# A decoder layer on one core: order of loads at the start of the down stage, and order of copies in the first gate matrix

## The chip, the core and the metric

The kernel runs on one core of a Trainium2 chip. The metric is device time in microseconds (us). The engines named below are TensorE (PE, with PEld for its weight loads), VectorE (DVE), ScalarE (ACT), GpSimd (POOL) and SyncE (SP), which here only issues DMAs; SPq is its queue.

## The reference

One inference step of a one-layer hybrid decoder: 1024 prompt tokens and 32 sample tokens (1056 columns in the kernel), width 1024. Attention and a recurrent mixer come first, then a gated feed-forward part of width 2816. Only that part is touched:

```python
def conv_ffn(h, buf, w_gate, w_up, conv_w, conv_b, w_down):
    T = h.shape[1]
    a = h @ w_gate
    ext = jnp.concatenate([buf.astype(a.dtype), a], axis=1)
    c = conv_b + sum(conv_w[j] * ext[:, j:j + T] for j in range(CONV_W))
    y = (jax.nn.silu(c) * (h @ w_up)) @ w_down
    return y, ext[:, -(CONV_W - 1):]
...
xp = xp + mixer_out(...)
y, cbuf_p = conv_ffn(rms_norm(xp, norm2_g[l]), buf0, w_gate[l], w_up[l], conv_w[l], conv_b[l], w_down[l])
xp = xp + y
```

## The kernel before, in words

Everything is float32. Each operand of a product is split into a high part (ScalarE, a copy to a shorter format) and a low part (the rest: VectorE for tokens, GpSimd for weights), and each product is three matmuls: high by high, high by low, low by high. Each engine works through its own list in the order written; semaphores join them.

The feed-forward part is computed in block products of Strassen's kind (Winograd's form): seven products in place of eight. There are 11 groups of 256 hidden features, and each has a gate matrix and an up matrix of seven items (`matrix`, L2386 and on). An item runs for two halves `z` of 264 columns; its result stays in one of three pairs of PSUM banks, "a", "b", "c" (roles `acababa`). `copies` (ScalarE) takes the result of items 0, 2 and 3 out to SBUF; `c11`, `c22` and `c12` (VectorE) add it to other banks, and `bank_free` holds TensorE until a bank may be written: item 5 waits for the copy of item 3 (`w5_ready`), item 6 for `c22`.

**The gate seam** is the first group's gate matrix. There the token operands of items 2 to 6 are still being made (`x_high` on ScalarE, `x_low` on VectorE; steps 20 to 23 are B22 for item 5, steps 24 to 27 are T4 for item 6, from `make_t4`), and so is the norm's root: `log_of(1)`, `log_of(2)` read PSUM banks, `root` follows, and VectorE waits for it (`rb_ready`) before it scales the gates. TensorE's transpose of the old gates behind item 5 waits for all three logs (`ln_ready`), since it writes one of their banks. GpSimd's next work waits for `make_t4`.

**The down stage** has 154 steps `s` (`B_STEPS`), 11 to a run `r`, 14 runs; run `r` is product `p = r // 2`, half `z = r % 2`. A step is 12 matmuls of 264 columns. It needs a weight quad (one for two steps, loaded by `down_weights`, split by ScalarE and GpSimd) and a token piece: `acts_in(s)` loads it into one of 8 stages, `act_high(s)` (ScalarE) and `act_low(s)` (VectorE) split it into one of 8 operand buffers. In runs 2 and 3 a piece has two parts (264 KB in place of 132), and VectorE forms their difference first (`t_sum`). Both engines work 6 steps ahead (`AHEAD`), VectorE's `t_sum` 8 steps. SyncE issues the pieces 12 steps ahead, each behind the low part of the piece 8 before it (`tl_ready`). At the end of a run VectorE adds the PSUM banks to the residual (`evict`). The residual `acc` lies where the operands T3 and T4 were, so it comes back from memory (`residual_back`) behind the last up matrix. The last group's products are stored and read back (`products`, `p_stored`), and the sums of its down weights are formed from three loaded blocks (`sum_sources`, then `down_sums` on VectorE, then `sums_out`).

Of the kernel before, what the change touches and what calls it, by code (L numbers as in the profile page):

```python
# [29 lines left out]
TT = T + NS  # L30
NT = T // P
NPC = 3
PW = TT // NPC
# [1823 lines left out]
GROUPS = FC // G2  # L1857
HF = TT // 2
ZW = HF // 2
KH = KC // 2  # L1860
# [95 lines left out]
def tail(nc, io, keep, room, at):  # L1956
# [7 lines left out]
    with ExitStack() as ctx:  # L1964
        sb, ps, sem = open_memory(nc, ctx, keep["sems"])
# [103 lines left out]
        th_ready, tl_ready, b_ready = sem("th_ready"), sem("tl_ready"), sem("f_b_ready")  # L2069
        r_in = [sem(f"r_in{n}") for n in range(2)]  # L2070
        be_ready, yt_ready, ye_ready, yd_ready = sem("be_ready"), sem("yt_ready"), sem("ye_ready"), sem("yd_ready")
# [16 lines left out]
        with nc.Block() as block:  # L2088
            @block.sync
            def _(sp):  # L2090
# [68 lines left out]

                def residual_back(side):  # L2160
                    if side == 0:
                        sp.wait_ge(res_stored[0], 16)
                    else:
                        sp.wait_ge(res_stored[2], 16 * KH)
                        sp.wait_ge(res_stored[3], 16 * KH)
                    sp.wait_ge(res_stored[1], 16)
                    cols = slice(side * HF, (side + 1) * HF)
                    sp.dma_start(acc[:, :, cols], io["x_d"][:, :, cols]).then_inc(r_in[side], 16)

# [71 lines left out]
                sp.wait_ge(p_ready, p_use(MATS - 1, 6, 1))  # L2241
                residual_back(0)
                acts_in(8), acts_in(9)
                sum_sources(GROUPS - 1)
                sp.wait_ge(p_stored, 16 * GROUPS)
                acts_in(10), acts_in(11)
                residual_back(1)
                sums_out(GROUPS - 1)
                for s in range(B_STEPS):
                    r, f = divmod(s, GROUPS)  # L2250
                    if s + 12 < B_STEPS:
                        acts_in(s + 12)
                    q = quad_at(s)
                    if s >= 4 and q is not None and q + 4 < B_QUADS:
                        down_weights(q + 4)
                    if r - 1 in DONE and f == 9:
                        outputs(r - 1)
# [233 lines left out]
            def _(act):  # L2491
# [197 lines left out]
                def gate_matrix(m, g, first):  # L2689
# [12 lines left out]
                    if first:  # L2702
                        for i in range(20, 24):
                            x_high(i)
                        log_of(1), log_of(2), root(slice(PW, TT))
                        copies(m, g, 0, 3, True, False)
                        for i in range(24, 28):
                            x_high(i)
                    next_quad(m, g, 0, 2, False)
                    if not first:  # L2710
# [50 lines left out]
                for s in range(B_STEPS):  # L2761
                    r, f = divmod(s, GROUPS)
# [15 lines left out]
            def _(dve):  # L2778
# [171 lines left out]
                def group(g, first, link, last=False):  # L2950
# [5 lines left out]
                    if first:  # L2956
                        for i in range(20, 24):
                            x_low(i)
                        for j in range(KH):
                            make_t4(j)  # L2960
                        for i in range(24, 28):
                            x_low(i)
                        dve.wait_ge(rb_ready, 2)
                    c22(m, 0, gates[1])
                    dve.wait_ge(c22_ready, m * 2 + 2)
# [37 lines left out]
                def evict(r, block, j):  # L3003
                    h, side = BLOCKS[r // 2][block]
                    z = r % 2
                    if r in (0, 2) and j == 0:
                        dve.wait_ge(r_in[r // 2], 16)
                    if r >= 4 and block == 0 and j == 0:
# [7 lines left out]
                for s in range(B_STEPS):  # L3016
# [3 lines left out]
                    if s + AHEAD < B_STEPS:  # L3020
                        act_low(s + AHEAD)
                    if s == 2:
                        down_sums(GROUPS - 1)
# [132 lines left out]
```

## Time and profile before

| | us |
|---|---|
| median of three runs | 1471.75 (1470.19 to 1478.22) |
| the profiled execution | 1464.73 |
| its span | 1463.0 |
| TensorE busy | 1402.4 |
| VectorE busy | 997.1 |
| ScalarE busy | 712.7 |
| GpSimd busy | 630.7 |

Mean granted TensorE clock: 0.983 of full speed. The gate and up matrices run from about 733 us to 1215 us, the down stage from there to 1457 us. Matmuls overlap, so the start of one to the start of the next (0.12 us for 264 columns at full clock) is what counts, not the length shown.

### The profile page before, as it was taken

The numbers are of one execution on the slowest core, as the hardware profiler recorded it, in microseconds if no ns is written. First come the engines' busy times: TensorE is split into PE (matmuls) and PEld (weight loads), VectorE is DVE, ScalarE is ACT, GpSimd is POOL, SyncE is SP. The second block draws the span as 40 slices with busy tenths as digits, with TensorE's granted clock in tenths as the row PEclk, the third lists the DMA queues.
The fourth block names the chain that finished last, engine by engine and source line by source line (L and its number), as shares of the span: only waits on it lengthen the run. The fifth ranks groups of instructions, "written<-read, shape, count | busy, mean of one in ns | idle before, by whom it ended". The sixth has DMA issues, their size and how long they took to land.

```text
span 1463.0 us, 27919 instructions
## 1 busy us (share of the span) xinstructions
PE 1402.4 (96%) x10382; PEld 1329.4 (91%) x10382; DVE 997.1 (68%) x1698; ACT 712.7 (49%) x1412; POOL 630.7 (43%) x408
## 2 busy tenths in 40 slices
PE   6999999999999998999988999999999997999998
PEld 5888989798979897869988999999999997999998
DVE  6558555855585458756499777777788775976952
ACT  5537544745564456364364444434444443544452
POOL 0000300030003000423149889999999973544840
PEclk9999999999999899999999999999999998999999
DMA  8221103110311030846311443343223348966762
GB/s 276 94 73 30 39 22 103 29 45 17 103 43 30 17 102 16 249 134 213 118 50 31 132 130 131 103 130 131 81 95 116 131 154 293 316 186 192 248 208 76
DMA packets 174952, 171.41 MB, mean 117 GB/s; under 512 B 9351, under 2 KB 144908, under 8 KB 174860
## 3 DMA queue, kind: packets, MB, share of 16 engines
q1 hardware_dynamic: 173614, 169.38, 36.9%
q8 instruction: 59, 0.97, 0.3%
q10 hardware_dynamic: 1246, 0.79, 0.2%
q14 instruction: 33, 0.27, 0.1%
HBM read 125.75 MB, written 44.39 MB: 116 GB/s over the span
## 4 chain that ended last, share of the span: by engine, by line
PE 47%; DVE 4%; issue 2%; DMA 1%; SPq 0%; POOL 0%; ACT 0%; POOLq 0%; DVEq 0%; ACTq 0%
PE f_up L2324 8%; PE f_up L2326 8%; PE f_up L2325 8%; PE f_gp L2324 7%; PE f_gp L2326 7%; PE f_gp L2325 7%; PE f_dn L2324 1%; PE f_dn L2325 1%; PE f_dn L2326 1%; DMA m_raw<-w_out 1%; DMA f_ksum<-w_down 1%; DVE f_conv L2920 1%; DVE f_conv L2913 0%; DVE f_conv L2916 0%; DVE f_act L2926 0%
## 5 line engine op out<-in xcount | busy, mean ns | idle before, releaser
L143 PE MATMUL z_ps<-h_hi,w_hi 128*128 128x352 f32 x600 | 202.5, 337 | 0.0
L145 PE MATMUL z_ps<-h_hi,w_lo 128*128 128x352 f32 x600 | 194.7, 324 | 0.0
L144 PE MATMUL z_ps<-h_lo,w_hi 128*128 128x352 f32 x600 | 194.3, 324 | 0.0
L2291 POOL TENSOR_TENSOR f_qlo<-f_raw,f_qhi 128x512 fp32r<-128x512 f32 x88 | 149.2, 1705 | 41.2 <-ACT f_qhi L2585 24.0
L2295 POOL TENSOR_TENSOR f_bring<-f_braw,f_bring 128x512 fp32r<-128x512 f32 x77 | 108.0, 1407 | 106.9 <-ACT f_bring L2616 106.8
L578 POOL TENSOR_TENSOR room<-room 128x1056 f32<-128x1056 f32 x4 | 9.7, 2434 | 321.5 <-ACT room L1235 321.5
L2291 POOL TENSOR_TENSOR f_qlo<-f_sum,f_qhi 128x512 fp32r<-128x512 f32 x66 | 130.4, 1987 | 15.7 <-ACT f_qhi L2585 15.7
L2926 DVE TENSOR_TENSOR f_act<-f_stage,f_act 128x264 fp32r<-128x264 f32 x132 | 88.7, 693 | 58.3 <-ACT f_act L2629 58.3
L143 PEld LDWEIGHTS z_ps<-h_hi,w_hi 128*128 128x128 f32 x600 | 114.3, 191 | 1.8 <-issue 1.3
L144 PEld LDWEIGHTS z_ps<-h_lo,w_hi 128*128 128x128 f32 x600 | 114.8, 191 | 0.3
L145 PEld LDWEIGHTS z_ps<-h_hi,w_lo 128*128 128x128 f32 x600 | 114.1, 190 | 0.0
L573 POOL TENSOR_TENSOR room<-room 128x512 f32<-128x512 f32 (+1 forms) x28 | 30.4, 1087 | 179.4 <-DVE room L1465 104.8
L2629 ACT ACTIVATE f_act<-f_stage 128x264 fp32r<-128x264 f32 x132 | 54.8, 422 | 107.0 <-PE f_gp L2326 37.4
L1079 ACT ACTIVATE room<-z_ps 128x352 f32<-128x352 f32 x81 | 37.2, 459 | 133.9 <-PE z_ps L145 125.4
L2585 ACT ACTIVATE f_qhi<-f_raw 128x512 fp32r<-128x512 f32 x88 | 54.8, 625 | 84.7 <-PE f_up L2326 44.1
L2324 PE MATMUL f_gp<-f_act,f_bring 128*128 128x264 f32 x231 | 66.7, 289 | 0.0
L2325 PE MATMUL f_gp<-f_act,f_bring 128*128 128x264 f32 x231 | 66.2, 287 | 0.0
L2326 PE MATMUL f_gp<-f_act,f_bring 128*128 128x264 f32 x231 | 66.2, 286 | 0.0
L2324 PE MATMUL f_up<-f_act,f_bring 128*128 128x264 f32 x231 | 65.7, 284 | 0.0
L2325 PE MATMUL f_up<-f_act,f_bring 128*128 128x264 f32 x231 | 65.5, 284 | 0.0
L2326 PE MATMUL f_up<-f_act,f_bring 128*128 128x264 f32 x231 | 65.5, 283 | 0.0
L2585 ACT ACTIVATE f_qhi<-f_sum 128x512 fp32r<-128x512 f32 x66 | 41.2, 627 | 37.3 <-PE f_up L2326 31.3
(462 smaller groups left out, 5027.9 us busy)
## 6 DMA issues: line engine op xcount, KB each, us to landing
f_stage<-a_d SPq DMA_DIRECT2D x132, 132.0 KB, 3.1
w_raw<-w_in SPq DMA_DIRECT2D x28, 512.0 KB, 4.0
a_d<-f_u SPq DMA_DIRECT2D x11, 1056.0 KB, 8.8
f_raw<-w_gate SPq DMA_DIRECT2D x22, 512.0 KB, 6.1
f_raw<-w_up SPq DMA_DIRECT2D x22, 512.0 KB, 5.1
f_braw<-w_down SPq DMA_DIRECT2D x44, 256.0 KB, 3.6
f_ksum<-w_down SPq DMA_DIRECT2D x33, 256.0 KB, 3.2
s_d<-f_ksum SPq DMA_DIRECT2D x11, 768.0 KB
```

Of the source, the lines that this page charges most:

```text
L143: nc.tensor.matmul(out, whi[:, k, :], hi[:, k, :], start=(k == 0), stop=False)
L144: nc.tensor.matmul(out, whi[:, k, :], lo[:, k, :], start=False, stop=False)
L145: last = nc.tensor.matmul(out, wlo[:, k, :], hi[:, k, :], start=False, stop=(k == chunks - 1))
L1079: return a(dst[:, piece(n)], bank_of(k)[:, 0:PW], ACT.Copy)
L2291: tt(qlo[i][:, :, :], source(b, i), qhi[i][:, :, :].bitcast(F32), ALU.subtract).then_inc(aw_ready, 1)
L2295: tt(ring[q % SLOTS][:, 1, :, :], braw[q % 8][:, :, :], ring[q % SLOTS][:, 0, :, :].bitcast(F32), ALU.subtract).then_inc(aw_ready, 1)
L2324: mm(out, wh, xh, start=first, stop=False, skip_group_check=goes_on)
L2325: mm(out, wh, xl, start=False, stop=False, skip_group_check=goes_on)
L2326: return mm(out, wl, xh, start=False, stop=last, skip_group_check=goes_on)
L2585: a(qhi[i][:, :, :], source(b, i), ACT.Copy).then_inc(ah_ready, 1)
L2629: a(acts[s % 8][:, 0, :], src, ACT.Copy).then_inc(th_ready, 1)
L2926: v.tensor_tensor(acts[s % 8][:, 1, :], src, acts[s % 8][:, 0, :].bitcast(F32), ALU.subtract).then_inc(tl_ready, 1)
```

## The change

In the down stage, SyncE's list is put in another order: pieces 8 and 9, the wait for the stored products and pieces 10 and 11 come before any residual; the residual comes in four blocks (rows 0 to 3 and rows 4 to 7 of the eight, left and right half) at the head and in steps 5, 12 and 15; the sum sources are loaded in step 1, their sums stored in step 9, and VectorE makes them in its step 5 in place of step 2. The waits of `evict` follow. In the gate seam, ScalarE's copies of item 3 and `x_high` 24 to 27 come before the two logs and the root, and VectorE's `c22` before `x_low` 24 to 27.

```diff
--- before.py
+++ after.py
@@ -2067,7 +2067,7 @@
         braw_in = [sem(f"braw_in{s}") for s in range(8)]
         st_in = [sem(f"st_in{s}") for s in range(STAGES)]
         th_ready, tl_ready, b_ready = sem("th_ready"), sem("tl_ready"), sem("f_b_ready")
-        r_in = [sem(f"r_in{n}") for n in range(2)]
+        r_in = [sem(f"r_in{n}") for n in range(3)]
         be_ready, yt_ready, ye_ready, yd_ready = sem("be_ready"), sem("yt_ready"), sem("ye_ready"), sem("yd_ready")
         y_stored = [sem(f"y_stored{s}") for s in range(YBUFS)]
 
@@ -2157,15 +2157,15 @@
                     else:
                         sp.dma_start(stage[s % STAGES][:, 0, :], io["a_d"][2 * f + (p in (4, 5, 6)), :, cols]).then_inc(st_in[s % STAGES], 16)
 
-                def residual_back(side):
+                def residual_back(h, side):
                     if side == 0:
                         sp.wait_ge(res_stored[0], 16)
                     else:
                         sp.wait_ge(res_stored[2], 16 * KH)
                         sp.wait_ge(res_stored[3], 16 * KH)
                     sp.wait_ge(res_stored[1], 16)
-                    cols = slice(side * HF, (side + 1) * HF)
-                    sp.dma_start(acc[:, :, cols], io["x_d"][:, :, cols]).then_inc(r_in[side], 16)
+                    rows, cols = slice(KH * h, KH * h + KH), slice(side * HF, (side + 1) * HF)
+                    sp.dma_start(acc[:, rows, cols], io["x_d"][:, rows, cols]).then_inc(r_in[2 if h else side], 16)
 
                 def outputs(r):
                     h, tiles = DONE[r]
@@ -2239,15 +2239,22 @@
                 products(GROUPS - 1)
                 down_weights(14)
                 sp.wait_ge(p_ready, p_use(MATS - 1, 6, 1))
-                residual_back(0)
                 acts_in(8), acts_in(9)
-                sum_sources(GROUPS - 1)
                 sp.wait_ge(p_stored, 16 * GROUPS)
                 acts_in(10), acts_in(11)
-                residual_back(1)
-                sums_out(GROUPS - 1)
+                residual_back(0, 0)
                 for s in range(B_STEPS):
                     r, f = divmod(s, GROUPS)
+                    if s == 1:
+                        sum_sources(GROUPS - 1)
+                    if s == 5:
+                        residual_back(0, 1)
+                    if s == 9:
+                        sums_out(GROUPS - 1)
+                    if s == 12:
+                        residual_back(1, 0)
+                    if s == 15:
+                        residual_back(1, 1)
                     if s + 12 < B_STEPS:
                         acts_in(s + 12)
                     q = quad_at(s)
@@ -2702,10 +2709,10 @@
                     if first:
                         for i in range(20, 24):
                             x_high(i)
-                        log_of(1), log_of(2), root(slice(PW, TT))
                         copies(m, g, 0, 3, True, False)
                         for i in range(24, 28):
                             x_high(i)
+                        log_of(1), log_of(2), root(slice(PW, TT))
                     next_quad(m, g, 0, 2, False)
                     if not first:
                         copies(m, g, 0, 3, False, False)
@@ -2958,10 +2965,12 @@
                             x_low(i)
                         for j in range(KH):
                             make_t4(j)
+                        c22(m, 0, gates[1])
                         for i in range(24, 28):
                             x_low(i)
                         dve.wait_ge(rb_ready, 2)
-                    c22(m, 0, gates[1])
+                    else:
+                        c22(m, 0, gates[1])
                     dve.wait_ge(c22_ready, m * 2 + 2)
                     v.tensor_tensor(gates[1][:, right], gates[1][:, right], total[:, right], ALU.mult).then_inc(gr_ready, 1)
                     c12(m, 0, gates[0])
@@ -3003,8 +3012,8 @@
                 def evict(r, block, j):
                     h, side = BLOCKS[r // 2][block]
                     z = r % 2
-                    if r in (0, 2) and j == 0:
-                        dve.wait_ge(r_in[r // 2], 16)
+                    if r in (0, 2, 4) and block == 0 and j == 0:
+                        dve.wait_ge(r_in[r // 2], 32 if r == 4 else 16)
                     if r >= 4 and block == 0 and j == 0:
                         dve.wait_ge(be_ready, e_count(r - 1))
                     dve.wait_ge(b_ready, b_use(GROUPS * r + GROUPS - 1, j))
@@ -3019,7 +3028,7 @@
                         t_sum(s + AHEAD + 2)
                     if s + AHEAD < B_STEPS:
                         act_low(s + AHEAD)
-                    if s == 2:
+                    if s == 5:
                         down_sums(GROUPS - 1)
                     if f == GROUPS - 1:
                         for block in range(len(BLOCKS[r // 2])):
```

## Rows read from the trace of the kernel before

**Rows 1.** The page, part 1: busy us, share, instructions.

```profile
PE 1402.4 (96%) x10382; PEld 1329.4 (91%) x10382; DVE 997.1 (68%) x1698; ACT 712.7 (49%) x1412; POOL 630.7 (43%) x408
```

**Rows 2.** Stretches: us, busy us by engine, clock, DMA share, GB/s.

```profile
1150.00:1200.00 50.00, 50.00 (x413) 49.96 (x412) 40.26 (x52) 22.70 (x44) 44.13 (x25) 1.00 0.33 109
1200.00:1250.00 50.00, 42.02 (x318) 41.16 (x317) 32.63 (x40) 19.56 (x45) 23.24 (x16) 0.90 0.84 279
```

**Rows 3.** TensorE's timeline, down seam: start, length, idle in brackets.

```profile
1218.41 0.36 PE L2324 MATMUL f_dn<-f_act,f_bring 128*128 128x264 f32 x1 [0.40 <-DVE f_act L2926]
...
1231.39 0.56 PE L2324 MATMUL f_dn<-f_act,f_bring 128*128 128x264 f32 x1 [3.99 <-DVE f_act L2926]
...
1237.20 0.56 PE L2324 MATMUL f_dn<-f_act,f_bring 128*128 128x264 f32 x1 [2.83 <-DVE f_act L2926]
...
1239.97 0.42 PE L2324 MATMUL f_dn<-f_act,f_bring 128*128 128x264 f32 x1
```

**Rows 4.** SyncE's queue in the same seam.

```profile
1216.89 0.40 SPq L2119 DMA_DIRECT2D a_d<-f_u  x1
...
1217.90 0.96 SPq L2168 DMA_DIRECT2D room<-x_d  x1
...
1236.73 0.34 SPq L2132 DMA_DIRECT2D s_d<-f_ksum  x1
```

**Rows 5.** Stretches of the seam: TensorE, clock, DMA share, GB/s.

```profile
1230.00:1235.00 5.00, 2.98 (x12) 0.51 1.06 391
...
1220.00:1235.00 15.00, 10.38 (x73) 0.84 1.03 364
1255.00:1275.00 20.00, 20.00 (x167) 1.00 1.02 344
```

**Rows 6.** Chain of waits, weight sums.

```profile
1222.04 10.69 DMA f_ksum<-w_down
1232.76 1.68 DVE f_ksum L2945
...
1236.11 0.60 DVE f_ksum L2948
```

**Rows 7.** DMA issues: count, KB each, us to landing (first: page).

```profile
f_stage<-a_d SPq DMA_DIRECT2D x132, 132.0 KB, 3.1
...
f_stage<-a_d SPq DMA_DIRECT2D x22, 264.0 KB, 4.9
...
room<-x_d SPq DMA_DIRECT2D x2, 2112.0 KB, 12.6
a_d<-f_u SPq DMA_DIRECT2D x1, 1056.0 KB, 5.2
```

**Rows 8.** TensorE's timeline, gate seam.

```profile
764.87 0.56 PE L2324 MATMUL f_gp<-f_b22h,f_qhi 128*128 128x264 f32 x1 [4.32 <-issue]
```

**Rows 9.** ScalarE's timeline, gate seam.

```profile
757.47 2.61 ACT L2556 ACTIVATE f_b22h<-room,vec 128x528 fp32r<-128x528 f32 x4
...
764.40 0.37 ACT L2647 ACTIVATE f_pw<-f_gp 128x264 f32<-128x264 f32 x1
```

**Rows 10.** VectorE's timeline, gate seam.

```profile
752.43 2.56 DVE L2822 TENSOR_TENSOR f_t1l<-f_t1f,f_t1h 128x528 fp32r<-128x528 f32 x4
...
761.08 2.80 DVE L2814 SCALAR_TENSOR_TENSOR room<-room,vec,f_t2f 128x528 f32<-128x528 f32 x4
765.62 6.51 DVE L2822 TENSOR_TENSOR f_t<-room,f_t 128x528 fp32r<-128x528 f32 x4 [1.74 <-ACT f_t L2554]
772.06 0.76 DVE L2887 TENSOR_TENSOR f_gate<-f_gp,f_pw 128x264 f32<-128x264 f32 x2
...
777.30 0.43 DVE L2973 TENSOR_TENSOR f_gate<-f_gp,total 128x264 f32<-128x264 f32 x1 [0.86 <-PE f_gp L2326]
```

**Rows 11.** GpSimd's timeline, gate seam.

```profile
763.96 2.51 POOL L2291 TENSOR_TENSOR f_qlo<-f_raw,f_qhi 128x512 fp32r<-128x512 f32 x2 [17.24 <-DVE room L2814]
```

**Rows 12.** TensorE's timeline, end of the up matrix.

```profile
796.66 0.36 PE L2324 MATMUL f_up<-f_t,f_qhi 128*128 128x264 f32 x1 [1.65 <-DVE f_u L2887]
```

## The prediction

> **What bounds the kernel now.** The page comes first: TensorE is busy for 1402.4 of 1463.0 us [rows 1], so only stretches in which it stands or runs slowly can give time back. The busy time by stretches finds them. From 1150 to 1200 us the engine runs 413 matmuls in 50 us, from 1200 to 1250 only 318 [rows 2]: 95 are missing, at 50/413 = 0.121 us each 11.5 us. A step of the down stage has 12 matmuls, so it takes 1.453 us. TensorE's own timeline places the loss. Step 2 starts at 1218.41; then 3.99 us idle ahead of 1231.39 (step 8) and 2.83 us ahead of 1237.20 (step 9); step 10 starts at 1239.97 [rows 3]. Undisturbed, it would start at 1218.41 + 8 x 1.453 = 1230.0. So 9.9 us are lost by then, with step 10's first two matmuls, still slow, 10.1. Part of it is clock: step 9's 12 matmuls take from 1237.20 to 1239.97, 0.23 us each, and the granted clock is 0.51 then, the lower of the levels 1.2 and 2.4 GHz, after 3.99 us of idling [rows 3, 5].
>
> SyncE's queue says why. At 1217.90 it issues the whole left residual (2112 KB), only then pieces 8 and 9, the sum sources, pieces 10 and 11, and the right residual; pieces 12 on must wait until the weight sums are stored, at 1236.73 [rows 4]. The chain shows the second hold: sources landed after 10.69 us, three VectorE sums up to 1236.71, and only behind them on VectorE the low part of piece 9 [rows 6]. The DMA engines are full all the while: 364 GB/s at a share of 1.03 from 1220 to 1235, and still 344 GB/s at 1.02 from 1255 to 1275 [rows 5].
>
> The second place is the first group's gate matrix: 4.32 us idle ahead of item 5 at 764.87 [rows 8], and a shorter idle stretch ahead of item 6.
>
> **The down stage.** The queue at 1217.9 becomes: pieces 8, 9; the wait for the stored products; pieces 10, 11; a residual block of 1056 KB; then within the loop the sources (s=1), three more blocks (s=5, 12, 15) and the sums' store (s=9). DMAs on SyncE go from 2 residual issues to 4 (0.34 to 0.96 us of issue each [rows 4]); nothing else is added.
>
> Pieces 8 and 9 now have only the product store and 256 KB of weights ahead of them. Behind a queue that short I take the 3.1 us that a small piece has over the whole run [rows 7], counted from the store's landing at 1216.89 + 5.2 = 1222.1 [rows 4, 7] as the late bound: 1225, ahead of step 8 at 1218.41 + 6 x 1.453 = 1227.1. The 3.99 us go, and with them the 2.83 us and the slow clock.
>
> What is late next: the sums. VectorE takes them up after the low part of piece 11, and the low part of piece 12 is queued behind them, then all later ones. Ahead of the last source's landing lie, from 1222.2 on, pieces 10 to 12, one block and 768 KB of sources: 0.41 + 1.08 + 0.79 = 2.27 MB. The first piece lands at 1222.2 + 3.1 = 1225.3, the remaining 2.14 MB at 364 GB/s take 5.9 us: 1231.2. Before, the sums took 1236.71 - 1232.76 = 3.95 us [rows 6]; the shortest of the three took 0.6, so three of that length are 1.8, the other end. GpSimd slows them (below) and works on one weight quad in every two steps, so not all of the time: I take 3.3. With 0.4 us for the low part, step 12 can start at 1234.9 in place of 1218.41 + 10 x 1.453 = 1232.9: a new stall of 2.0 us. Ends: 0 (sources one us early, sums in 2.0 us) and 3.7 (one us late, 3.95 us). The clock should hold: 1.65 us idle at 796.66 left the first matmul at 0.36 us, where a slow one has 0.56 [rows 3, 12].
>
> Next, the DMA engines. The same bytes are moved, and before they were full until 1275. What PE gained must come out of load lead. From step 22 a piece is 264 KB, and VectorE forms a difference of piece n before the low part of piece n-2. So step 25 needs piece 27, the first behind all four blocks. From 1222.2 up to it: pieces 10 to 21, 1.62 MB; 22 to 27, 1.62; blocks 4.33; sources and store of sums 1.57; six weight loads 1.57; in all 10.71 MB, at 364 GB/s 29.4 us. With the first piece landing after 3.1 us and the other 10.57 MB after that it ends at 1222.2 + 3.1 + 29.0 = 1254.3; two VectorE operations on 264 columns (0.4 each, as the additions in [rows 10]) put step 25 at 1255.1. Undisturbed it would be 1251.8, with the 2.0 us stall 1253.8. Before it was 1239.97 + 0.2 + 15 x 1.453 = 1262.0. So the down stage gives 6.9 us. At 391 GB/s, the best five microseconds [rows 5], the stream ends 2 us earlier, the sums' stall rules and it gives 8.2; at 344, 5.2. The lower end is 5, the upper the whole 10.1. I stay at 6.9, on the rate of the same seam. Later steps need 0.27 + 0.13 MB each, 1.1 us at that rate against 1.453: no further stall. The residual's first block is needed at step 10's end and the last at step 54's: both long landed.
>
> The Trainium skill (DMA: Bandwidth & Descriptors, Bandwidth) gives about 358 GB/s as a core's share of HBM and 435 as the fabric's ceiling. The trace lies at 364 to 391, so the first is nearer; by it the stream ends 0.5 us later than in my sum, by the second the DMA engines would bind nowhere.
>
> **The gate seam.** ScalarE is free at 757.47 + 2.61 = 760.1 and then does a table load, two logs, another table load and a root before the two copies at 764.40 [rows 9], 4.3 us in all; item 5 starts as the first is done. Moved ahead, the copies end at 760.75, and item 5 starts behind item 4 at 764.87 - 4.32 = 760.55. It takes 24 x 0.121 = 2.9 us and ends at 763.5. But item 6 needs the low parts of T4. VectorE's make_t4 ends at 761.08 + 2.80 = 763.9 as before; the two c22 additions now come next (0.76 us [rows 10]), then the four lows from 764.6. Their high parts are then there, as ScalarE makes them from 761.8 on instead of after the root. They took 6.51 us at 765.62, while GpSimd worked without pause from 763.96, but 2.56 at 752.43, when it had nothing to do [rows 10, 11]. GpSimd starts on make_t4's signal, which doesn't move, so 6.5 us: 771.1 in place of 772.1. The logs and the root move behind x_high(27), which ends 0.65 us [rows 9] after make_t4, at 764.5; the same 4.3 us put the root's end at 768.8 and the logs' earlier. TensorE's transpose after item 5 waits for the logs, so some 3 us in which only the first T4 rows could run: hidden behind the lows. If item 6 then runs its last 15 matmuls slowly, it ends at 771.1 + 15 x 0.23 = 774.5, against 777.2 before, when VectorE's product waited for it [rows 10]. VectorE, from the end of the lows (c22, before, ended at 772.8) to the start of its last product at 777.30 less 0.86 of waiting, had 3.6 us of work; so 771.1 + 3.6 = 774.7, and with that product's 0.4 it is at 775.1 against 777.7 [rows 10]. Both are 2.6 to 2.7 us ahead. VectorE has no gap from there to 796.66, where TensorE waits 1.65 us for it [rows 12], so its advance is what arrives; with 0.1 off for TensorE's last slow matmuls -2.5. Ends: 0 (something in the next matrix, such as GpSimd's unmoved sums, holds both) and -4.3 (the whole first wait). VectorE needs the root at 771.1, after its end. No table load is added: the order log, root, later activations stays.
>
> The Trainium skill (GPSIMD Engine Reference, Specifications) says that GpSimd shares its SBUF interfaces with VectorE and that instructions with two SBUF inputs contend. The trace agrees (6.51 against 2.56 us). It speaks against expecting the whole 4.3 us: without it the lows would end at 767.2, and PE, waiting for the logs, would gain some 4.
>
> **Sum.** -6.9 - 2.5 = -9.4 us. The profiled execution took 1464.73 us (span 1463.0 and 1.7 around it), so 1455.3 by its own measure. The median of the three runs is 1471.75, 7.0 above it; set against that the forecast is 1462.4. What is under 0.5% (7.4 us) I call no change.
>
> **The rivals.** (A) No new stall: sums and stream come in time, 10.1 + 2.5 = 12.6, 1459.2. For it: the DMA windows reach 391 GB/s; against it: VectorE's order and the full DMA share. 0.17. (B) The DMA engines, not the order, set step 22 on: full from 1218 to 1275 on both sides, so nothing in the down stage comes back, only -2.5: 1469.3. Against it: from 1240 to 1275 SyncE ran ahead of TensorE, so there is lead to spend. 0.12. (C) The gate seam gives nothing, since GpSimd's sums or the transpose's wait for the logs eat it: -6.9, 1464.9. 0.13. (D) Slower: the two late blocks fall among the 264 KB pieces. SyncE may load piece n only after the low part of piece n-8, and that stands six steps behind the difference for piece n-2; so a landing time above 6 x 1.453 = 8.7 us sets the pace. Residuals took 12.6 us to land, the 264 KB pieces 4.9 [rows 7]. Were they at 12.6 for all 22 steps, each six cost 3.9 us more: 14.3, with the slow clock about 18; less 12.6 that is +5: 1477. It decides from 8.7 us on. 0.08. My own case has 0.50, with a range of 1459 to 1466.
>
> **How the numbers follow.** Faster: most of my case, A and a part of C, 0.65. Same: the rest of mine, B and half of C, 0.27. Slower: D, 0.08. The range goes from A less the 1.6 us between the lowest run and the median to just above B, and leaves out D: 1457.5 to 1470.
>
> **What would show it.** Right: no idle ahead of step 8; one gap of about 2 us ahead of step 12, ended by VectorE's low part behind the sums; granted clock 1.00 from 1220 to 1245; landing of 264 KB pieces under 8.7 us; first copies of item 3 at about 760.1, item 6's end near 774.5. Wrong: a gap at steps 20 to 30 of more than 3 us, a half clock there, or a transpose that starts after the T4 lows.

## The result and the profile after

The changed kernel takes 1461.84 us (median of 8 runs, 1454.68 to 1464.88) against 1472.52 us for the kernel before in the same rounds (8 runs, 1468.88 to 1478.22): ratio 0.9931, 95% interval 0.9913 to 0.9949. Two more series of it gave 0.9941 (0.9915 to 0.9967) and 0.9947 (0.9919 to 0.9974). The prediction was 1462.4 us, range 1457.5 to 1470. The profiled execution took 1461.8 us, its span is 1460.0.

The page, part 1, of the kernel after (busy us, share, instructions; compare [rows 1]):

```profile
PE 1408.9 (97%) x10382; PEld 1334.8 (91%) x10382; DVE 1009.4 (69%) x1698; ACT 713.5 (49%) x1412; POOL 639.9 (44%) x408
```

The two profiled spans differ by only 3.0 us, less than the change gives. The reason lies in a half that the change doesn't touch. The stretches (us, busy us and instructions of PE, PEld, DVE, ACT, POOL, then granted clock, DMA share, GB/s), first of before, then of after:

```profile
200.00:300.00 100.00, 96.60 (x655) 85.68 (x655) 62.92 (x140) 62.60 (x129) 6.67 (x6) 1.00 0.20 60
```

```profile
200.00:300.00 100.00, 96.72 (x620) 85.14 (x621) 63.12 (x141) 59.75 (x123) 2.43 (x1) 0.95 0.20 60
1200.00:1250.00 50.00, 46.71 (x368) 46.09 (x367) 37.93 (x50) 21.83 (x48) 26.29 (x18) 0.97 0.83 280
1220.00:1235.00 15.00, 14.60 (x121) 14.42 (x120) 8.74 (x11) 4.11 (x10) 7.41 (x6) 1.00 0.92 299
1235.00:1240.00 5.00, 2.86 (x20) 2.65 (x19) 5.00 (x8) 2.57 (x7) 2.71 (x2) 0.88 1.07 394
1240.00:1245.00 5.00, 5.00 (x34) 5.00 (x34) 3.41 (x8) 2.45 (x6) 2.58 (x2) 0.77 1.04 385
```

From 200 to 300 us this execution was granted 0.95 of the clock and ran 35 matmuls fewer than the one of before (655 and 620). Item 5 of the first gate matrix starts at 766.80 here; before it could have at 764.87 - 4.32 = 760.55 [rows 8]. So everything below is read from marks inside each trace: **the gate part** runs from the moment at which item 5's operands are there and item 4 has ended (its first matmul; where that waited for the copy, less the wait) to step 2 of the down stage, **the down part** from step 2 to the span's end. Before, they are 1218.41 - 760.55 = 457.86 and 1463.0 - 1218.41 = 244.59. After, they are 454.14 and 239.06: 3.7 and 5.5 us less, 9.25 in all.

TensorE's timeline of the kernel after (start, length, idle in brackets; compare [rows 3, 8, 12]):

```profile
766.80 0.36 PE L2331 MATMUL f_gp<-f_b22h,f_qhi 128*128 128x264 f32 x1
...
773.36 0.30 PE L2389 MATMUL f_dn<-ident,f_scr 128*128 128x128 f32 x1 [3.41 <-ACT total L2517]
775.58 0.59 PE L2331 MATMUL f_gp<-f_t,f_qhi 128*128 128x264 f32 x1 [1.07 <-DVE f_t L2829]
777.27 0.59 PE L2331 MATMUL f_gp<-f_t,f_qhi 128*128 128x264 f32 x1 [0.66 <-DVE f_t L2829]
...
800.53 0.36 PE L2331 MATMUL f_up<-f_t,f_qhi 128*128 128x264 f32 x1 [1.58 <-DVE f_u L2894]
...
1220.94 0.36 PE L2331 MATMUL f_dn<-f_act,f_bring 128*128 128x264 f32 x1 [0.40 <-DVE f_act L2933]
...
1237.90 0.39 PE L2331 MATMUL f_gp<-f_act,f_bring 128*128 128x264 f32 x1 [2.14 <-DVE f_act L2933]
...
1263.47 0.36 PE L2331 MATMUL f_dn<-f_act,f_bring 128*128 128x264 f32 x1 [0.35 <-DVE f_act L2933]
```

Item 5 waits for nothing. In the place of its wait stand 3.41 us ahead of the transpose (for ScalarE's logs) and 1.07 and 0.66 us inside item 6 (for the T4 lows). In the down stage the waits ahead of steps 8 and 9 are gone; one of 2.14 us stands ahead of step 12 (1237.90), and step 28 (1263.47) waits a little. The other engines around the two seams, VectorE first (compare [rows 6, 10]):

```profile
770.14 0.77 DVE L2894 TENSOR_TENSOR f_gate<-f_gp,f_pw 128x264 f32<-128x264 f32 x2
770.82 6.39 DVE L2829 TENSOR_TENSOR f_t<-room,f_t 128x528 fp32r<-128x528 f32 x4
...
781.10 0.76 DVE L2982 TENSOR_TENSOR f_gate<-f_gp,total 128x264 f32<-128x264 f32 x2
...
1234.51 0.69 DVE L2952 TENSOR_TENSOR f_ksum<-f_ksum 128x512 f32<-128x512 f32 x1 [3.47 <-DMA f_ksum<-w_down]
...
1236.32 3.98 DVE L2933 TENSOR_TENSOR f_act<-f_stage,f_act 128x264 fp32r<-128x264 f32 x5
...
1257.23 0.43 DVE L2942 TENSOR_TENSOR f_t2raw<-f_stage 128x264 f32<-128x264 f32 x1 [2.37 <-DMA f_stage<-a_d]
```

GpSimd starts its next two operations 0.52 us ahead of VectorE's lows (compare [rows 11]):

```profile
770.30 2.96 POOL L2298 TENSOR_TENSOR f_qlo<-f_raw,f_qhi 128x512 fp32r<-128x512 f32 x2 [17.25 <-DVE room L2821]
```

ScalarE (compare [rows 9]):

```profile
766.32 0.38 ACT L2654 ACTIVATE f_pw<-f_gp 128x264 f32<-128x264 f32 x1
...
768.21 2.69 ACT L2561 ACTIVATE f_t<-room 128x528 fp32r<-128x528 f32 x4 [1.24 <-DVE room L2821]
770.92 1.28 ACT L2517 ACT_TABLE_LOAD   x1
772.21 1.00 ACT L2517 ACTIVATE total<-f_dn,eps 128x352 f32<-128x352 f32 x2
```

And SyncE's queue (compare [rows 4]): pieces 8 and 9 go before the first residual block, and the queue never stands for the sums again.

```profile
1219.43 0.40 SPq L2119 DMA_DIRECT2D a_d<-f_u  x1
...
1220.43 4.82 SPq L2158 DMA_DIRECT2D f_stage<-a_d  x4
1225.34 1.20 SPq L2168 DMA_DIRECT2D room<-x_d  x1
...
1228.31 0.47 SPq L2128 DMA_DIRECT2D f_ksum<-w_down  x1
...
1238.72 0.43 SPq L2132 DMA_DIRECT2D s_d<-f_ksum  x1
...
1242.47 0.40 SPq L2168 DMA_DIRECT2D room<-x_d  x1
...
1246.18 0.47 SPq L2168 DMA_DIRECT2D room<-x_d  x1
```

### The profile page after: what moved, and what is told of

It is laid out like the page before. It is cut to its first block, busy times and chain, and to the rows that moved or that the text cites. A ratio compares the mean times of both kernels' runs of the same rounds, so it can differ in the third digit from the quotient of the medians.

```text
span 1460.0 us, 27925 instructions
## 1 busy us (share of the span) xinstructions
PE 1408.9 (97%) x10382; PEld 1334.8 (91%) x10382; DVE 1009.4 (69%) x1698; ACT 713.5 (49%) x1412; POOL 639.9 (44%) x408
## 4 chain that ended last, share of the span: by engine, by line
PE 44%; DVE 3%; issue 3%; POOL 2%; DMA 2%; ACT 1%; SPq 0%; DVEq 0%; ACTq 0%; POOLq 0%
PE f_up L2331 8%; PE f_up L2333 8%; PE f_up L2332 7%; PE f_gp L2333 6%; PE f_gp L2331 6%; PE f_gp L2332 6%; POOL f_qlo L2298 1%; PE f_dn L2331 1%; PE f_dn L2332 1%; PE f_dn L2333 1%; DMA f_stage<-a_d 1%; DMA f_ksum<-w_down 1%; DVE f_act L2933 0%; DMA a_d<-f_u 0%; DVE f_t2f L2812 0%
## 5 line engine op out<-in xcount | busy, mean ns | idle before, releaser
L2298 POOL TENSOR_TENSOR f_qlo<-f_raw,f_qhi 128x512 fp32r<-128x512 f32 x88 | 152.9, 1748 | 36.8 <-ACT f_qhi L2592 19.1
L2302 POOL TENSOR_TENSOR f_bring<-f_braw,f_bring 128x512 fp32r<-128x512 f32 x77 | 114.4, 1493 | 95.1 <-ACT f_bring L2623 95.0
L2933 DVE TENSOR_TENSOR f_act<-f_stage,f_act 128x264 fp32r<-128x264 f32 x132 | 94.5, 738 | 40.4 <-ACT f_act L2636 40.4
```

Source lines behind the costliest of these rows:

```text
L2298: tt(qlo[i][:, :, :], source(b, i), qhi[i][:, :, :].bitcast(F32), ALU.subtract).then_inc(aw_ready, 1)
L2302: tt(ring[q % SLOTS][:, 1, :, :], braw[q % 8][:, :, :], ring[q % SLOTS][:, 0, :, :].bitcast(F32), ALU.subtract).then_inc(aw_ready, 1)
L2933: v.tensor_tensor(acts[s % 8][:, 1, :], src, acts[s % 8][:, 0, :].bitcast(F32), ALU.subtract).then_inc(tl_ready, 1)
```

## The experiments

Every trace is cut at the same marks, one trace to a kernel. "None listed" means that the trace names no wait there, "one run" that the kernel was run once and has no ratio. The old orders are read as one group, the new ones as another:

| kernel | gate part | down part | idle ahead of step 12 | ratio to before (95%) |
|---|---|---|---|---|
| before | 457.86 | 244.59 | (3.99 + 2.83 earlier) | |
| after | 454.14 | 239.06 | 2.14 | 0.9931 (0.9913 to 0.9949) |
| e1_down | 457.85 | 239.16 | 1.89 | 0.9950 (0.9924 to 0.9977) |
| e2_gate | 453.79 | 245.75 | (3.81 + 2.84 earlier) | 0.9973 (0.9949 to 0.9996) |
| e3_sources_first | 453.64 | 239.37 | none listed | 0.9937 (0.9914 to 0.9961) |
| e4_blocks_late | 455.49 | 235.21 | none listed | 0.9912 (0.9884 to 0.9940) |
| e5_blocks_late_only | 453.5 | 235.60 | 0.84 | one run |
| e6_gpsimd_later | 456.15 | 239.10 | 2.26 | 0.9924 (0.9892 to 0.9955) |
| e7_logs_between | 457.1 | 239.34 | 2.02 | one run |
| e8_c22_back | 456.4 | 239.23 | 0.95 | one run |
| f1_blocks_late_timed | 454.9 | 238.37 | 2.02 | 0.9931 (0.9903 to 0.9960) |
| f2_after_timed | 455.3 | 239.53 | 2.02 | 0.9941 (0.9915 to 0.9967) |
| f3_order_best_timed | 455.8 | 236.09 | 1.08 | 0.9915 (0.9884 to 0.9946) |
| f4_after_paired | 453.6 | 239.21 | 2.15 | 0.9947 (0.9919 to 0.9974) |

### The two halves of the change by themselves: e1_down and e2_gate

The first is the changed kernel with the old gate seam, the second the kernel before with the new one:

```diff
# e1_down
-                        copies(m, g, 0, 3, True, False)
-                        for i in range(24, 28):
-                            x_high(i)
                         log_of(1), log_of(2), root(slice(PW, TT))
+                        copies(m, g, 0, 3, True, False)
+                        for i in range(24, 28):
+                            x_high(i)
...
-                        c22(m, 0, gates[1])
                         for i in range(24, 28):
                             x_low(i)
                         dve.wait_ge(rb_ready, 2)
-                    else:
-                        c22(m, 0, gates[1])
+                    c22(m, 0, gates[1])
```

> Down part of the change alone; the gate seam as before. Measured by the trace from step 2 of the down stage to the end of the span (before 244.6 us, whole change 239.1) and from the last matmul of item 4 in the first gate matrix to step 2 (before 458.1, whole change 454.3). My theory (two independent stalls): 239.1 and 458.1, so 5.5 us off the whole time. Rival (the down stage can only use what the DMA engines leave, and an earlier start of it counts): with the stage starting later by the missing gate gain, the down part would give more, over 7 us.

> Gate part alone; down stage as before. My theory: 454.3 from item 4 to step 2 (3.8 us gained, of which 2.5 by the end of the first up matrix and 1.3 later), 244.6 from step 2 on. Rival: the 1.3 us that came after the first up matrix are chance in how VectorE and GpSimd meet, and the gain is 2.5 (455.6). Whole time 2.5 to 3.8 us below before.

Each keeps its own part to 0.1 to 0.4 us: down alone 239.16, gate alone 453.79. e1's gate part is that of before (457.85). e2's down part is 245.75, 1.2 us above before: with almost the same two waits, its matmuls ran 0.22 us apart up to 1246.66, 6.1 us after the end of the second wait, where before had 3.2 us of that. So the parts add within that spread, and the down stage is the larger. e1's expectation held for both parts, e2's for the gate part; its down part is off by those 1.2 us. Over whole runs e1 is 7.0 and e2 3.2 us below before, where 5.5 and 2.5 to 3.8 were expected. e2's timeline has the old idle places:

```profile
1234.76 0.56 PE L2324 MATMUL f_dn<-f_act,f_bring 128*128 128x264 f32 x1 [3.81 <-DVE f_act L2926]
...
1240.58 0.56 PE L2324 MATMUL f_dn<-f_act,f_bring 128*128 128x264 f32 x1 [2.84 <-DVE f_act L2926]
```

e1's is the more telling one. Its stall ahead of step 12 is 1.89 us with the clock at 1.00, where the changed kernel had 2.14 us and 0.88 and 0.77 behind it; yet its down part is not shorter. What it saved there it lost behind 1260, where step 25 (1265.26) waits 0.69 us, with no such wait in the changed kernel. Step 28 (1270.59) waits as long as there, 0.36 us against 0.35:

```profile
1244.78 0.39 PE L2331 MATMUL f_gp<-f_act,f_bring 128*128 128x264 f32 x1 [1.89 <-DVE f_act L2933]
...
1265.26 0.36 PE L2331 MATMUL f_dn<-f_act,f_bring 128*128 128x264 f32 x1 [0.69 <-DVE f_act L2933]
1270.59 0.36 PE L2331 MATMUL f_dn<-f_act,f_bring 128*128 128x264 f32 x1 [0.36 <-DVE f_act L2933]
```

Step 28 starts 42.55 us after step 2 here and 42.53 us in the changed kernel. Whatever TensorE loses ahead of it, it arrives at the same time. e8 (below) agrees: 0.95 us ahead of step 12, and 239.23.

### Stall or stream: e3_sources_first, e4_blocks_late, e5_blocks_late_only

```diff
# e3: the sources ahead of the first block
+                sum_sources(GROUPS - 1)
                 residual_back(0, 0)
...
-                    if s == 1:
-                        sum_sources(GROUPS - 1)
# e5: the last two blocks behind the 264 KB pieces; e4: both edits
-                    if s == 12:
+                    if s == 33:
                         residual_back(1, 0)
-                    if s == 15:
+                    if s == 36:
                         residual_back(1, 1)
```

> Changed kernel with the sources of the weight sums loaded ahead of the first residual block instead of in step 1. Sources land some 3 us sooner, the sums are made before step 12 needs VectorE, so the 2.1 us idle ahead of step 12 and the slow clock behind it (2.0 us) go in both theories. My theory (DMA engines full, piece 27 is the floor): the same bytes stand ahead of piece 27, which landed 36.3 us after step 2, so a new idle stretch of about 3 us appears at steps 22 to 28 and the stage gains 0 to 1.5 us: 237.6 to 239.1. Rival (only the sums held the stage): all 4.1 us come back, 235.0.

> As the run before, and the last two residual blocks moved from steps 12 and 15 to steps 33 and 36, behind the 264 KB pieces; they are needed at step 54. My theory: with 2.2 MB less ahead of piece 27 the DMA floor is some 6 us lower and all idle of the stage goes: 234.6 to 235.5 from step 2 to the end, 4 us below the changed kernel. Rival (the DMA engines were never a floor): no different from the run before. A third way: the blocks now meet the product 2 and 3 loads and give a stall at steps 36 to 50.

> Changed kernel with only the last two residual blocks moved to steps 33 and 36; the weight sums as in the changed kernel, so the idle stretch of about 2 us ahead of step 12 stays. The run with both moves took 235.2 us from step 2 to the end. If the stall is paid once the stream of pieces is no floor any more: 237.3, or 239.3 where the clock falls after it as it did in the changed kernel (2.14 us idle, clock down to 0.77 over five us) but not in the down-only run (1.89 us idle, clock 1.00). Rival (the floor sits elsewhere, the late blocks gave nothing in the run with both): 239.1 without any fall of the clock.

e3 has no idle time listed ahead of step 12, and its down part is 239.37: removing the stall gave nothing. It came back in four waits at 1255.11 to 1266.81 (0.79, 0.86, 0.68 and 0.37 us, 2.7 in all, where about 3 were expected). e4, with 2.16 MB fewer ahead of piece 27, takes up that piece 30.67 us after step 2 in place of 36.29 (after, e1) and 36.55 (e3): 5.6 to 5.9 us, as 2.16 MB at 377 GB/s would be 5.7. The stall at steps 36 to 50 that its third way named did not come. Its down part is 235.21, close to the 234.5 that before would have without its 10.1 us of loss. The landing times in that stretch, after first (issued between 1219 and 1262), then e4 (1221 to 1262):

```profile
room<-x_d SPq DMA_DIRECT2D x4, 1056.0 KB, 7.8
f_stage<-a_d SPq DMA_DIRECT2D x14, 264.0 KB, 7.9
```

```profile
f_stage<-a_d SPq DMA_DIRECT2D x18, 264.0 KB, 5.1
```

e5 was to lose the step 12 stall of 2 us as before, 237.3 us. It had only 0.84 us of it and 235.60: the size missed, the sign held. The same kernel again (below) had 2.02 us and 238.37. What sets the two apart stands in the traces: how long the first low part behind the sums took. In the tile views it is 1519 ns in after (and 1518 in f1) and 425 ns in e5, and GpSimd's operation beside it goes the other way. First after, then e5:

```profile
L2933 DVE TENSOR_TENSOR f_act<-f_stage,f_act x1: 1519/1519/1519, 1236.3 to 1236.3; 128x264 fp32r<-128x264 f32 x1
L2302 POOL TENSOR_TENSOR f_bring<-f_braw,f_bring x1: 1272/1272/1272, 1236.3 to 1236.3; 128x512 fp32r<-128x512 f32 x1
```

```profile
L2933 DVE TENSOR_TENSOR f_act<-f_stage,f_act x1: 425/425/425, 1224.7 to 1224.7; 128x264 fp32r<-128x264 f32 x1
L2302 POOL TENSOR_TENSOR f_bring<-f_braw,f_bring x1: 1599/1599/1599, 1224.6 to 1224.6; 128x512 fp32r<-128x512 f32 x1
```

In all seven traces with a stall of 1.89 to 2.26 us GpSimd starts 0.04 us ahead of VectorE, and the low part takes 1.51 to 1.52 us. In e5 and e8 GpSimd is 0.03 and 0.01 us ahead, the low part takes 0.43 and the stall is 0.84 and 0.95. So 1.1 us of the stall hang on a few hundredths of a microsecond.

### The gate seam: e6_gpsimd_later, e7_logs_between, e8_c22_back

```diff
# e6: GpSimd behind the T4 lows in place of make_t4
-                pool.wait_ge(t4_ready, KH)
+                pool.wait_ge(xl_ready, len(X_STEPS))
# e7: only the copies ahead of the logs, x_high 24 to 27 behind the root
                         copies(m, g, 0, 3, True, False)
+                        log_of(1), log_of(2), root(slice(PW, TT))
                         for i in range(24, 28):
                             x_high(i)
-                        log_of(1), log_of(2), root(slice(PW, TT))
# e8: only ScalarE's order is new, c22 stays behind the lows
-                        c22(m, 0, gates[1])
                         for i in range(24, 28):
                             x_low(i)
                         dve.wait_ge(rb_ready, 2)
-                    else:
-                        c22(m, 0, gates[1])
+                    c22(m, 0, gates[1])
```

> Changed kernel; GpSimd's next work in the gate seam waits for the four T4 low parts instead of for make_t4. Theory (the two engines slow each other): the four lows take 2.6 us in place of 6.4, so item 6 ends 2 to 4 us sooner; GpSimd starts 3.2 us later and may then hold items 2 and 3 of the up matrix, so of that 1 to 2.5 us are left at step 2 (452 to 453 us from item 5 to step 2, against 454.1, 453.8, 453.6 and 455.5 in the four runs with the gate part). Rival (the lows are slow for themselves, or GpSimd sets the pace after the seam): lows still above 5 us, or no gain or a loss up to 3 us at step 2.

> Changed kernel with ScalarE's logs and root between the copies of item 3 and the four T4 high parts. TensorE's transpose no longer waits 3.4 us for the logs. Theory (that wait was hidden behind the T4 lows, VectorE's chain sets the pace): the first T4 high comes at about 5.2 us after item 5's start instead of 2, the lows start 1.2 us later and the part from item 5 to step 2 is 1.2 us longer. Rival (the transpose's wait is on the path): up to 3.4 us shorter.

> Changed kernel with VectorE's c22 behind the four T4 lows again; ScalarE's order as changed. Theory: item 6 can't start before c22, so its first nine matmuls no longer run between the lows; all 24 run from some 10.2 us after item 5's start at the slow clock, item 6 ends 1.6 us later and step 2 comes 1 to 1.6 us later. Rival (the copies alone made the gain): the same time as the changed kernel, 453.6 to 454.1 from item 5 to step 2.

**e6** shows the contention: with GpSimd idle the same four lows take 2.55 us in place of 6.39. It also shows what is late next. VectorE then waits 1.97 us for the root, and GpSimd's work comes 3.2 us later:

```profile
771.08 2.55 DVE L2829 TENSOR_TENSOR f_t<-room,f_t 128x528 fp32r<-128x528 f32 x4
775.60 1.19 DVE L2975 TENSOR_TENSOR f_gate<-f_gate,total 128x528 f32<-128x528 f32 x1 [1.97 <-ACT total L2521]
```

TensorE starts the up matrix 2.7 us sooner (11.20 us after item 5 in place of 13.94), as expected, but stands 2.60 us at 786.84 in it for ScalarE's copy. The gate part is 456.15, 1.7 us above the mean of the new order, where 452 to 453 was expected: on the time at step 2 the rival held.

**e7** separates the two moves on ScalarE. The copies alone free item 5, but the lows start 5.16 us after item 5 in place of 4.02, since the high parts come behind the root, and they take 6.50 us. The gate part is 457.1: of the mean 3.4 us of the new order 0.8 is left. The loss, 2.7 us against that mean, is more than the 1.2 expected, and not all of it need be the edit's. At the mark of [rows 12] e7 stands 34.81 us after item 5, the old order 36.1, the nine traces of the new order 32.55 to 33.73; behind it come waits that differ from trace to trace (below). The rival (up to 3.4 us shorter without the transpose's wait) fell. Much of the gain lies in the high parts of T4 being made ahead of the logs; how much, one trace doesn't show.

**e8** surprised. Without the two `c22` additions first, the lows took 2.55 us, though GpSimd was working; this time GpSimd's first two operations took 4.74 us where the changed kernel had 2.96. The lows start 0.16 us ahead of GpSimd here and 0.52 us behind it there. VectorE, then GpSimd:

```profile
766.77 2.55 DVE L2829 TENSOR_TENSOR f_t<-room,f_t 128x528 fp32r<-128x528 f32 x4
771.98 0.77 DVE L2894 TENSOR_TENSOR f_gate<-f_gp,f_pw 128x264 f32<-128x264 f32 x2 [2.65 <-ACT total L2521]
```

```profile
766.93 4.74 POOL L2298 TENSOR_TENSOR f_qlo<-f_raw,f_qhi 128x512 fp32r<-128x512 f32 x2 [17.23 <-DVE room L2821]
```

But `c22` stands behind the wait for the root, 8.6 us after item 5's start instead of 3.3, and item 6 waits for `c22`: the gate part is 456.4. So without the move of `c22` 2 us of the 3.4 are lost, by one trace of e8 against the mean of nine of the new order (1 to 1.6 was expected). At the mark of [rows 12] it is less: 34.16 us after item 5, 0.4 to 1.6 us later than the nine. The losses of e7 and e8 add to more than the whole gain (2.7 and 2.0 of 3.4), so they are no shares of it.

### Timed beside each other: f1 to f4

f1 is e5's kernel again, f3 is e4's, f2 and f4 are the changed kernel unedited, each pair in the same rounds.

> The changed kernel with its third and fourth residual block issued in steps 33 and 36 in place of 12 and 15, timed in five rounds; its one run so far cannot be set apart from its undisturbed first half. Theory (the DMA stream up to piece 27 sets the seam, so 2.16 MB less ahead of it give 3.5 us from step 2 to the end): step 2 to span end 235.6 us as in the one look, against 239.1 for the changed kernel; median 3.5 us below the changed kernel's 1461.8, so about 1458.3, ratio to the kernel before 0.9905. Rival (the low 1446.9 of the one look was due to this order): a median below 1452, ratio under 0.987.

> The changed kernel as it is, in the same rounds as the version with the blocks late, for a comparison on one chip. Theory: step 2 to span end 239.1 to 239.4 us, item 5 to step 2 within 453.5 to 455.5; ratio to the kernel before 0.993 to 0.994, and 3.5 us above the version with the late blocks. Rival (the late blocks are worth nothing over whole runs): the two medians within 1 us of each other.

> The version with the sum sources ahead of the first residual block and the last two blocks in steps 33 and 36, timed again in five rounds beside the changed kernel. Theory (the stall ahead of step 12 and the DMA floor at step 25 are separate, and only this version is rid of both): no idle above 0.4 us ahead of step 12, step 2 to span end 235.0 to 235.5 us, against 239.1 to 239.5 for the changed kernel; over whole runs 3 to 4 us below the changed kernel of the same rounds. Rival (the remaining stall is a matter of chance of each execution, as between the two looks at the version with only the late blocks: 0.84 us and 2.02 us with a slow clock behind): idle of 1 us or more ahead of step 12 here too, 237 us or more from step 2 to the end, and a median within 2 us of the changed kernel's.

> The changed kernel as it is, in the same rounds. Theory: 239.1 to 239.5 us from step 2 to the end, about 2 us idle ahead of step 12, and a median 3 to 4 us above the version beside it. Rival: within 2 us of it.

f1: 1459.96 us (median of 10), f2: 1462.20 (12); f3: 1458.90 (8), f4: 1462.47 (12). e5's 1446.9 was not due to its order: f1's median lies within 0.2% of the other three. But f1's expectation failed as well: its down part is 238.37 in place of 235.6, its ratio 0.9931 in place of 0.9905, and f2 is 2.2 us above it in place of 3.5. (f2's own down part, 239.53, is 0.1 above its range.) Its stall was 2.02 us, and the clock fell behind it:

```profile
1235.00:1240.00 5.00, 2.98 (x16) 2.77 (x16) 5.00 (x8) 2.58 (x7) 2.68 (x2) 0.77 1.07 392
1240.00:1245.00 5.00, 5.00 (x39) 5.00 (x39) 3.01 (x7) 2.18 (x6) 2.58 (x2) 0.89 1.04 391
```

Here no floor hides this: 238.37 - 235.60 = 2.8 us, of which 1.2 is the longer stall (the slow low part of piece 12) and 1.6 the clock: f1 ran 16 matmuls 0.22 us apart in place of 0.12 from 1237.49 on. f3 had 1.08 us idle ahead of step 12, now behind the landing of piece 12 itself (issued 1229.7, taken up 1237.59), and 236.09, so its theory missed on both marks in the trace. Its rival had named 1 us and more there but also 237 us and a gain under 2 us; the medians differ by 3.6 us, as the theory had it. f4's expectation held. Over e4 and f3 the version stands at 0.9912 and 0.9915, the changed kernel at 0.9931, 0.9941 and 0.9947. The traces show 3 to 4 us between them in the down part; the intervals of the ratios overlap, so the whole-run gain is likely and not proved. It has the lowest ratio of all that were run.

## Why the prediction was right, point by point

**The sum held for the wrong split.** It was 6.9 + 2.5 = 9.4 us; the profiled pair shows 5.5 + 3.7 = 9.25. Each term was off by over a microsecond, in opposite directions; that they cancel is luck. Over all traces the old down order gives 244.59 and 245.75, the new one 239.06 to 239.53; the old gate order 457.86 and 457.85, the new one 453.5 to 455.8 in nine traces, mean 454.5. That is 5.9 and 3.4 us: the same 9.3. The medians of the same rounds differ by 10.7 us; the forecast of 1462.4 us is nearer than that since it was set against 1471.75, and before had 1472.52 in these rounds.

**The stalls ahead of steps 8 and 9** went, as said, and so did the half clock there.

**The new stall ahead of step 12** was forecast at 16.5 us after step 2 and came at 16.96. Three errors nearly cancel, which is luck too. The sources were taken up 13.57 us after step 2, not 12.8. The sums took 1.8 us (1234.51 to 1236.32), not 3.3: GpSimd stood idle from 1233.99 to 1236.28, and nothing slowed them. But the low part of piece 12, put at 0.4 us, took 1.5 beside GpSimd. In VectorE's tile view of after, the five low parts behind the sums have two kinds (minimum, median, maximum in ns):

```profile
L2933 DVE TENSOR_TENSOR f_act<-f_stage,f_act x5: 420/422/1519, 1236.3 to 1239.9; 128x264 fp32r<-128x264 f32 x5
```

A sum of 3.98 us is two of 1.5 and three of 0.4 with their overlaps, and the first is one of the long ones, as step 12 starts 1.58 us after it.

**"The clock should hold"** was wrong. It fell to 0.88 and 0.77 of full speed after the 2.14 us stall in the profiled run, and in f1 after 2.02; it held at 1.00 after 2.02 in f2, 2.15 in f4, 1.89 in e1, 2.02 in e7 and 2.26 in e6. The 1.65 us of [rows 12] that the sentence rested on was shorter than all of these. It cost nothing in the changed kernel only because the stream set the end anyway.

**The stream of loads** was sized well up to its last step. Piece 27 was taken up 36.29 us after step 2, forecast 35.9 (1254.3 - 1218.41). Two errors nearly cancel in that: from 1227.8, where the first piece should land, to 1257.2 the engines moved 375 GB/s, so 11.0 MB (some of it may belong to loads behind piece 27), where the sum has 10.57 MB at 364:

```profile
1227.80:1257.20 29.40, 27.26 (x212) 27.05 (x210) 18.15 (x28) 11.13 (x26) 13.82 (x11) 0.94 1.05 375
```

Step 25 came at 37.2 to 37.6 in e1, f2 and f4 (1265.26 - 1228.04 in e1), forecast 36.7. The term that was mis-sized is the sentence "no further stall": step 28 should have come at 41.0 and came at 42.5 to 43.0. Of f4's 1.6 us, 0.7 are there by step 25 and 0.9 come between steps 25 and 28. VectorE in f4 shows them:

```profile
1260.09 0.43 DVE L2942 TENSOR_TENSOR f_t2raw<-f_stage 128x264 f32<-128x264 f32 x1 [0.65 <-DMA f_stage<-a_d]
1260.44 1.53 DVE L2933 TENSOR_TENSOR f_act<-f_t2raw,f_act 128x264 fp32r<-128x264 f32 x1
1261.89 0.42 DVE L3021 TENSOR_TENSOR room<-room,f_gp 128x264 f32<-128x264 f32 x1
1262.23 1.09 DVE L3021 TENSOR_TENSOR room<-room,f_up 128x264 f32<-128x264 f32 x3
```

The difference of piece 29 waits 0.65 us for its landing, the low part of piece 27 takes 1.5 us, and then the eviction of run 1 (four additions, 1.4 us) stands in front of piece 28. With load lead these cost nothing (before had the same four additions at 1259.78 and no wait of TensorE behind them); with none, each is paid. The working counted bytes and left out VectorE's own list. That the floor is the stream is shown by e1 and e3 (stall or clock gone, same end) and by e4 (fewer bytes ahead, 4 us less).

**The rates.** From 1240 to 1262 us f4 moved 377 GB/s:

```profile
1240.00:1262.00 22.00, 21.11 (x170) 20.55 (x168) 13.44 (x27) 8.61 (x19) 8.43 (x6) 1.00 1.06 377
```

The Trainium skill (DMA: Bandwidth & Descriptors, Bandwidth) puts a core's share of HBM at about 358 GB/s, with both cores of an HBM domain streaming. The kernel runs on one core; its measured stretch, which holds writes and reads, is above the share, and the measurement decides.

**The gate seam** worked as described: item 5 unhindered, the transpose's wait for the logs hidden behind the lows, the lows again at 6.39 us against the 6.5 taken, starting 4.02 us after item 5, forecast 764.6 - 760.55 = 4.05. VectorE's last product ends 15.06 us after item 5 (781.10 + 0.76 - 766.80) against 17.18 before, 2.1 us ahead; 2.6 was forecast. The up matrix starts 13.94 us after item 5, where item 6's end was forecast 13.95 after it (774.5 - 760.55). At 800.53 the wait is 1.58 us, as in [rows 12], and the mark there is 33.73 us after item 5, against 36.11 before: 2.4 us. Four traces of the new order have 33.7 there, the other five 32.6, which would be 3.5 us. The rest of the 3.7 comes behind it: before has waits of 0.69, 0.20 and 0.66 us at 803.42, 839.27 and 846.00, after has none. Such waits, up to 1.96 us in the second group's up matrix, differ from trace to trace of the same code, and with them the gate part, by 2.2 us. What sets them was not tried.

**The rivals.** A (no new stall) fell: six of the seven traces of the new down order have 1.89 to 2.26 us of stall, the seventh 0.95 (e8). B (nothing in the down stage) fell by e1; its mechanism, the full DMA engines, is what keeps 4 of the 10 us. C fell by e2. D did not come as a slower kernel, but its mechanism did, in small: the 264 KB pieces took 7.9 us to land (median; 4.9 before [rows 7]), and single ones more than the 8.7 from which it decides. Piece 27, issued at 1246.70 just behind the fourth block (1246.18), was taken up 10.5 us later. e4 moved that block and the third one away, and the wait went with them. That shows B's mechanism and D's together; no run tells one from the other.

## What to carry to other kernels

Behind a stall that is removed stands the next floor, so price it to the end of its reach: not only the bytes up to the first late piece, but every operation of the engine that works them up, evictions included, until the lead is back. Where DMA engines are full, order alone moves a stall; bytes put behind the stretch (here two residual blocks needed much later) shorten it. When two engines share a resource, freeing one of them pays only if nothing else is due at the same moment.

## What was not expected of the hardware

The same pause of TensorE, about 2 us, brought the lower clock in two traces (2.14 and 2.02 us idle; granted clock down to 0.77 over 5 us) and not in five (1.89, 2.02, 2.02, 2.15, 2.26 us). Without a floor behind it, it cost 1.6 us. What sets the two apart from the five was not found.

Contention between VectorE and GpSimd can fall on either side. With the same operations, started within 0.6 us of each other, four VectorE operations on 528 columns took 6.39 us and two GpSimd operations 2.96 in the changed kernel; in e8 they took 2.55 and 4.74. The Trainium skill (GPSIMD Engine Reference, Specifications) says that the two share SBUF interfaces, which both cases bear out. Which side pays was not the same, and the traces point to who starts first. In the twelve traces in which GpSimd has started before the lows (by 0.52 us or more) they took 6.39 to 6.51 us; in e8, the one in which the lows start first, by 0.16 us, they took 2.55. Ahead of step 12 the turn lies between 0.04 and 0.03 us of lead for GpSimd (above). No run was made to test this.

The half of the program ahead of the change differs between executions by up to 14 us at the mark of item 5 (756.0 in e5, 770.4 in e3), with the clock at 1.00 and 0.95 from 200 to 300 us in these two. A change of 10 us can't be read from two spans.
